# One decoder layer with a routed mixture of experts on one core: the order of small products, of the first output units and of the first and last expert bodies

## What is computed

```python
xn = rms_norm(x, norm1_w)
qa, ka, va, qg, kg, vg, rg, gdown, gate_a, gate_g = split(xn @ w_in)
y_attn = swa_with_sinks(rope(rms_norm(qa)), rope(rms_norm(ka)), va) @ w_attn_branch
gk = log_sigmoid(gdown @ gla_gate_up + gla_gate_bias) / 16
og = rms_norm(gla_chunked(qg, kg, vg, gk)) * silu(rg)
y_gla = og @ w_gla_branch
merged = sigmoid(gate_a) * y_attn + sigmoid(gate_g) * y_gla
h = x + merged @ w_out
xn2 = rms_norm(h, norm2_w)
# one group of 4, then the best two of its 8 experts for each token
y = sum over the chosen experts of weight * ((silu(xn2 @ w_gate) * (xn2 @ w_up)) @ w_down)
out = h + y
```

## Time and profile before

| | us |
|---|---|
| median of 3 runs | 716.54 |
| lowest and highest | 716.33 and 716.84 |
| the profiled execution | 722.02 |
| its span, first to last instruction | 719.8 |
| PE busy within the span | 689.4 |
| DVE, ACT, POOL busy | 378.4, 207.4, 99.6 |

### The profile page before, as it was taken

The page is one execution under the profiler, slowest core; times in us unless marked ns, Lnnn a source line. Parts: engine busy times, 40 slices in busy tenths (PEclk is TensorE's granted clock), DMA queues, the critical chain, the costliest instruction groups (busy, mean ns, idle before and its releaser), DMA issues.

```text
span 719.8 us, 11191 instructions
## 1 busy us (share of the span) xinstructions
PE 689.4 (96%) x4523; PEld 533.1 (74%) x4523; DVE 378.4 (53%) x673; ACT 207.4 (29%) x443; POOL 99.6 (14%) x131
## 2 busy tenths in 40 slices
PE   3999999999999999999989987999999999999997
PEld 1579999878788888888779987665657575756655
DVE  3647224648987777785683454251525344241514
ACT  4355123214443434342433342112020202110111
POOL 1400006857700000000000011110101001010000
PEclk9999999999999999999999995999999999999998
DMA  7413112301111111113345028799999999999922
GB/s 225 136 58 118 60 59 67 110 1 59 59 60 60 59 58 60 59 60 117 117 155 226 30 101 339 294 411 387 412 382 384 404 373 407 392 416 381 416 113 117
DMA packets 49221, 139.32 MB, mean 194 GB/s; under 512 B 6002, under 2 KB 28035, under 8 KB 40980
## 3 DMA queue, kind: packets, MB, share of 16 engines
q1 hardware_dynamic: 46722, 134.36, 49.3%
q0 software_dynamic: 2304, 4.20, 1.7%
q10 hardware_dynamic: 146, 0.07, 0.1%
HBM read 138.61 MB, written 4.19 MB: 198 GB/s over the span
## 4 chain that ended last, share of the span: by engine, by line
PE 88%; DVE 5%; ACT 3%; DMA 2%; issue 2%; POOL 0%; ACTq 0%; DVEq 0%; POOLq 0%
PE bank L861 16%; PE bank L570 13%; PE bank L571 12%; PE bank L572 12%; PE bank L944 9%; PE bank L874 8%; PE bank L771 2%; DVE y_lo L1632 1%; PE bank L833 1%; PE bank L826 1%; PE bank L744 1%; PE bank L770 1%; PE bank L704 1%; PE bank L769 1%; PE bank L708 1%
## 5 line engine op out<-in xcount | busy, mean ns | idle before, releaser
L1327 DVE TENSOR_TENSOR wlo<-wraw,whi 128x2048 fp32r<-128x2048 f32 (+1 forms) x26 | 58.7, 2259 | 31.4 <-ACT whi L1053 31.4
L570 PE MATMUL bank<-whi,xhi 128*128 128x256 f32 (+1 forms) x256 | 73.8, 288 | 0.0
L572 PE MATMUL bank<-whi,xlo 128*128 128x256 f32 (+1 forms) x256 | 72.2, 282 | 0.0
L571 PE MATMUL bank<-wlo,xhi 128*128 128x256 f32 (+1 forms) x256 | 72.1, 282 | 0.0
L570 PE MATMUL bank<-xhi,whi 128*128 128x512 f32 (+2 forms) x176 | 69.3, 398 | 1.6 <-DVE wlo L1327 1.6
L571 PE MATMUL bank<-xlo,whi 128*128 128x512 f32 (+2 forms) x176 | 68.2, 391 | 0.0
L572 PE MATMUL bank<-xhi,wlo 128*128 128x512 f32 (+2 forms) x176 | 67.9, 390 | 0.0
L861 PE MATMUL bank<-wgate,xgT 128*64 128x256 f32 x512 | 59.0, 383 | 0.0
L861 PE MATMUL bank<-wup,xgT 128*64 128x256 f32 x512 | 58.4, 381 | 0.0
L874 PE MATMUL bank<-wdown,hT 128*64 128x512 f32 x256 | 58.1, 595 | 0.0
L1622 DVE SCALAR_TENSOR_TENSOR hg<-bank,pair_w,hs 128x256 f32<-128x256 f32 x16 | 7.7, 484 | 94.2 <-ACT hs L1257 94.2
(11 more groups left out here) (283 smaller groups left out, 1328.6 us busy)
## 6 DMA issues: line engine op xcount, KB each, us to landing
wgate<-in_expert_w_gate SPq DMA_DIRECT2D x32, 1024.0 KB, 8.0
wup<-in_expert_w_up SPq DMA_DIRECT2D x32, 1024.0 KB, 10.2
wdown<-in_expert_w_down SPq DMA_DIRECT2D x32, 1024.0 KB, 16.5
wraw<-in_w_in SPq DMA_DIRECT2D x17, 1024.0 KB, 5.5
wraw<-in_w_out SPq DMA_DIRECT2D x4, 1024.0 KB, 5.2
h<-in_x SPq DMA_DIRECT2D x4, 512.0 KB, 6.3
wraw<-in_w_gla_branch SPq DMA_DIRECT2D x2, 1024.0 KB, 5.0
wraw<-in_w_attn_branch SPq DMA_DIRECT2D x2, 1024.0 KB, 5.1
```

What stands on the lines that cost most here:

```text
L570: nc.tensor.matmul(ps, lhi(k), rhi(k), start=(k == 0), stop=False)
L571: nc.tensor.matmul(ps, lhi(k), rlo(k), start=False, stop=False)
L572: last = nc.tensor.matmul(ps, llo(k), rhi(k), start=False, stop=(k == kt - 1))
L1327: nc.vector.tensor_tensor(w_view(wlo[split_buffer(c)], c), w_view(wraw[c % 2], c), w_view(whi[split_buffer(c)], c).bitcast(F32), ALU.subtr ...
```

## The change

In `schedule()`:

- `("z",)` is split for PE: `("gates", 0)` after `("unit", 1, 1)`, `("gates", 1)` with the meta part after `("unit", 2, 0)`. ACT and DVE do their part of `z` after that, behind `("prep", 3)` instead of ahead of it.
- the units of chunks 8 and 9 are mixed, so that `attT` and `glao` stand behind different full units. The order in which ACT's results for `rg` are counted follows (`RG_ORDER`).

In the programs:

- the means of x for the next block are computed ahead of the scaling of a block;
- the output units (22, 0) and (23, 0) are computed together in `first_outputs`: slices 0 to 6 for both, then slice 7 for both;
- in the first body the transposes for s = 1, `slot_values(1)` and `onehot_transposes` come after the gate and up products of s = 0; DVE and ACT do their parts of it accordingly, and ACT takes the row numbers ahead of the one-hots. DVE builds both one-hots before it counts the rounds;
- in the last body `last_scatter` takes eight banks: the products of s = 0 for six units before the wait for `y_lo` of s = 1;
- `out` is stored in eight halves of blocks instead of four blocks.

```diff
+LAST_BANKS = (0, 1, 2, 3, 4, 5, 6, 7)
...
-    s += [("unit", 0, 0), ("xm", 1), ("unit", 1, 0), ("unit", 0, "m"), ("prep", 2), ("unit", 1, 1), ("z",)]
-    s += [("prep", 3), ("unit", 2, 0), ("unit", 2, 1), ("unit", 2, "m")]
+    s += [("unit", 0, 0), ("xm", 1), ("unit", 1, 0), ("unit", 0, "m"), ("prep", 2), ("unit", 1, 1), ("gates", 0)]
+    s += [("prep", 3), ("unit", 2, 0), ("gates", 1), ("z",), ("unit", 2, 1), ("unit", 2, "m")]
...
-    s += [("prep", 9)]
-    for b in range(NB):
-        s += [("unit", 8, b), ("attT", b)] + ([("kT",)] if b == 0 else [])
-        if b == 1:
-            s += [("qrope", 2)]
-        if b >= 1:
-            s += [("glao", b - 1)]
-    s += [("qrope", 3)]
-    s += [("prep", 10)]
-    for b in range(NB):
-        s += [("unit", 9, b)] + ([("glao", NB - 1)] if b == 0 else []) + [("qT", b), ("ognorm", b)]
+    s += [("prep", 9), ("unit", 8, 0), ("attT", 0), ("kT",), ("unit", 8, 1), ("attT", 1), ("qrope", 2)]
+    s += [("unit", 9, 0), ("glao", 0), ("qT", 0), ("qrope", 3), ("unit", 8, 2), ("attT", 2)]
+    s += [("unit", 9, 1), ("glao", 1), ("qT", 1), ("ognorm", 0), ("unit", 8, 3), ("attT", 3), ("prep", 10)]
+    s += [("unit", 9, 2), ("glao", 2), ("ognorm", 1), ("unit", 9, 3), ("qT", 2), ("glao", 3), ("ognorm", 2), ("qT", 3), ("ognorm", 3)]
...
+            def first_outputs():
+
+                pair = []
+                for c in (WO, WO + 1):
+                    pe.wait_ge(s_lo, c + 1)
+                    ps = banks.take(pe, "unit", ("unit", c, 0))
+                    pair.append((ps, w_view(whi[split_buffer(c)], c), w_view(wlo[split_buffer(c)], c)))
+                for ks in (range(KT - 1), (KT - 1,)):
+                    for ps, wh, wl in pair:
+                        for k in ks:
+                            pe.wait_ge(s_mhi, k + 1)
+                            nc.tensor.matmul(ps[:, 0:CW], mhi[:, k, 0:P], wh[:, k, :], start=(k == 0), stop=False)
+                            nc.tensor.matmul(ps[:, 0:CW], mhi[:, k, 0:P], wl[:, k, :], start=False, stop=False)
+                    for i, (ps, wh, wl) in enumerate(pair):
+                        for k in ks:
+                            pe.wait_ge(s_mlo, k + 1)
+                            last = nc.tensor.matmul(ps[:, 0:CW], mlo[:, k, 0:P], wh[:, k, :], start=False, stop=(k == KT - 1))
+                        if ks[-1] == KT - 1:
+                            last.then_inc(banks.done(("unit", WO + i, 0)), 1)
...
+                def last_scatter(i, n):
+
+                    def add_rows(u, s):
+                        b, half = u // 2, u % 2
+                        for part in (y_hi, y_lo):
+                            last = nc.tensor.matmul(tiles[LAST_BANKS[u]][:, :], onehotT[i % 3][s][:, b, :],
+                                                    part[s][:, half * 512:(half + 1) * 512], start=(s == 0 and part is y_hi),
+                                                    stop=(s == 1 and part is y_lo))
+                        if s == 1:
+                            last.then_inc(s_sc[u % 4], 1)
+
+                    pe.wait_ge(s_ylo[0], n + 1)
+                    for u in range(6):
+                        add_rows(u, 0)
+                    pe.wait_ge(s_ylo[1], n + 1)
+                    for u in range(6):
+                        add_rows(u, 1)
+                    for u in (6, 7):
+                        for s in range(2):
+                            add_rows(u, s)
...
-                row_transposes(0)
-                pe.wait_ge(s_pw, r * BODIES + 1)
-                slot_values(1)
-                for s in range(2):
-                    pe.wait_ge(s_ohT[s], r * BODIES + 1)
-                onehot_transposes()
+                row_transposes(0, (0,))
...
+                    if i == 0:
+                        row_transposes(0, (1,))
+                        pe.wait_ge(s_pw, n + 1)
+                        slot_values(1)
+                        for s in range(2):
+                            pe.wait_ge(s_ohT[s], n + 1)
+                        onehot_transposes()
...
-                        dve.wait_ge(s_sumsq, b + 1)
-                        nc.vector.tensor_scalar(stat[:, b:b + 1], stat[:, b:b + 1], 1.0 / D, EPS,
-                                                ALU.mult, ALU.add).then_inc(s_mean, 1)
+                        for ahead in (0, 1) if b == 0 else (b + 1,):
+                            if ahead < NB:
+                                dve.wait_ge(s_sumsq, ahead + 1)
+                                nc.vector.tensor_scalar(stat[:, ahead:ahead + 1], stat[:, ahead:ahead + 1], 1.0 / D, EPS,
+                                                        ALU.mult, ALU.add).then_inc(s_mean, 1)
```

More of the change, by code:

```diff
@@ L246 @@
 SCHEDULE = schedule()
+RG_ORDER = [step[1:] for step in SCHEDULE if step[0] == "unit" and CHUNKS[step[1]][0] == "rg"]
 def layer_kernel(nc, x, meta_tokens, norm1_w, w_in, q_norm_w, k_norm_w, attn_sinks, gla_gate_up, gla_gate_bias,
@@ L557, in _, with mm3 @@
         def _(pe):
-            def mm3(ps, lhi, llo, rhi, rlo, kt, merged=False):
-                if merged:
-                    for k in range(kt):
-                        pe.wait_ge(s_mhi, k + 1)
-                        nc.tensor.matmul(ps, lhi(k), rhi(k), start=(k == 0), stop=False)
-                        nc.tensor.matmul(ps, lhi(k), rlo(k), start=False, stop=False)
-                    for k in range(kt):
-                        pe.wait_ge(s_mlo, k + 1)
-                        last = nc.tensor.matmul(ps, llo(k), rhi(k), start=False, stop=(k == kt - 1))
-                    return last
+            def mm3(ps, lhi, llo, rhi, rlo, kt):
                 for k in range(kt):
@@ L606, in _ @@
                     name, c0, n, kt = CHUNKS[c]
+                    if c in (WO, WO + 1) and u == 0:
+                        if c == WO:
+                            first_outputs()
+                        continue
                     if u == 0:
@@ L636, in _ @@
                         last = mm3(ps[:, 0:n], cols(mhi, u * P, (u + 1) * P), cols(mlo, u * P, (u + 1) * P),
-                                   cols(wh, 0, n), cols(wl, 0, n), KT, merged=(c0 == 0 and u == 0))
+                                   cols(wh, 0, n), cols(wl, 0, n), KT)
                     last.then_inc(banks.done(step), 1)
-                elif kind == "z":
+                elif kind == "gates":
+                    j = step[1]
                     pe.wait_ge(s_const, (CONST_DMAS - EARLY_DMAS) * 16)
                     pe.wait_ge(*banks.emptied(("unit", 0, 0)))
+                    ps = banks.take(pe, "unit", ("z", j))
+                    nc.tensor.matmul(ps[:, :], gate_up[:, j * P:(j + 1) * P], gdT[:, NM:XC],
+                                     start=True, stop=True).then_inc(banks.done(("z", j)), 1)
+                    if j == 0:
+                        continue
                     pe.wait_ge(*banks.emptied(("unit", 0, "m")))
-                    for j in range(2):
-                        ps = banks.take(pe, "unit", ("z", j))
-                        nc.tensor.matmul(ps[:, :], gate_up[:, j * P:(j + 1) * P], gdT[:, NM:XC],
-                                         start=True, stop=True).then_inc(banks.done(("z", j)), 1)
                     ps = banks.take(pe, "T", "zm")
@@ L1013, in _ @@
                         reload(i, r * BODIES + i)
-            for b in range(NB):
-                for k in (2 * b % 4, 2 * b % 4 + 1):
-                    sp.wait_ge(s_add[k], rounds * (2 * BODIES) + b // 2)
-                sp.dma_start(out[0, b * P:(b + 1) * P, :], h[:, b, :]).then_inc(s_out, 16)
-            sp.wait_ge(s_out, 16 * NB)
+            for u in range(2 * NB):
+                b, cols_ = u // 2, slice(u % 2 * 512, (u % 2 + 1) * 512)
+                sp.wait_ge(s_add[u % 4], rounds * (2 * BODIES) + u // 4)
+                sp.dma_start(out[0, b * P:(b + 1) * P, cols_], h[:, b, cols_]).then_inc(s_out, 16)
+            sp.wait_ge(s_out, 16 * 2 * NB)
         @block.scalar
```

27 lines of the change are left out of this document (16 added, 11 removed).

## The result

| | before | after |
|---|---|---|
| first comparison, median (executions) | 716.69 (4) | 711.06 (4) |
| lowest and highest | 716.33 and 721.97 | 708.66 and 712.88 |
| beside the experiments, median | 720.92 (31), 721.87 (11), 720.78 (17) | 710.7 (6) |
| the profiled execution, its span | 722.02, 719.8 | 712.88, 711.0 |

A forecast was written before the change was run, and what follows sets the result against it. PE, busy 689.4 of 719.8 us, was taken as the bound, so only its waits and clock could change; 0.3 + 1.7 + 1.4 + 2.3 + 0.4 + 3.5 = 9.6 us off 716.54 gave 706.9, range 704.0 to 711.0.

The forecast's parts named there:

- The base: Whole kernel: the saving of 9.6 us is taken off the median 716.54, which lies 5.5 us under the profiled execution.
- Start: 0.3: Scalings of x: the mean computed ahead saves 0.3 us, as GpSimd's power stands still beside DVE's scaling; range to 1.6.
- more than the sum: Rival: GpSimd runs beside the scaling (1.3 more) and the clock rises early in the first body (0.7 more): 704.9; chance 0.13.
- Gate 1.7: Gate's wide products moved apart: the clock's fall from 47.5 to 50.9 goes, saving 1.7 us; range 0 to 1.7.
- gated attention 1.4: Chunks 8 and 9, units mixed: the clock's fall at 153.3 goes, saving 1.4 us; 0 with a new fall elsewhere.
- Output units 2.3: Units (22, 0) and (23, 0) together: unit (24, 0) starts 2.3 us earlier despite a new 1.7 us wait before hT; range 0.6 to 2.3.
- First body 0.4 saved: First expert body: gate and up of s = 0 ahead of the s = 1 transposes saves 0.4 us; 1.1 saved to 1.0 lost.
- L: First expert body: low-clock time in gate and up of s = 0, taken as 2.5 us; alternatives 1.15 and 5.5.
- Last body 3.5: Last expert body: the 2.1 us wait for y_lo and the 1.7 fall go; DVE's last sum starts 3.5 us earlier.
- The prediction's own sign of being wrong: Wrong if the clock falls where it was 1.00, PE waits for weights in the expert loop, or last eight sums exceed 5 us.
- Slower: Rival: attention from 180 to 330 us, shifted about 3.4 us earlier, gets new falls at 1.7 us each; chance 0.03.
- chance is in it: Rival, falls stay or move: each worth 1.4 to 1.7 us; two left 710.3, chance 0.25; all four 713.4, chance 0.05.

The follow-up runs named there:

- before_look: The kernel before, unchanged, profiled a second time; 720.96 us in a single execution.
- after_again: The changed kernel once more, unchanged; median 710.7 us beside 721.87 for the kernel before.
- fill_start: The changed kernel with idle PE products at the start, 6 ahead of a bank wait and 5 ahead of the first unit; 709.16 us.
- fill_gather: The changed kernel with idle PE products where PE waits for the choice of experts and the gather; 710.04 us.
- the medians of the four: Four kernels, each the kernel before with one part alone: last body, output units, gated attention, gate; medians 716.4, 717.86, 715.67, 715.36 us.
- outputs_only: The kernel before with only output units (22, 0) and (23, 0) computed together; median 717.86 us, ratio to before 0.998.
- gla_only: The kernel before with only the units of chunks 8 and 9 mixed; median 715.67 us, ratio to before 0.994.
- gate_only: The kernel before with only the gate's two wide products moved apart; median 715.36 us, ratio to before 0.995.
- before_late: The kernel before with seven idle PE products ahead of chunk 5's first unit; 719.7 us beside 720.78, ratio 1.000.

## Why the prediction was right or wrong

- **The base.** "The median lies 5.5 us under that execution, and I take the same saving off it." This step failed. Falls were treated as fixed parts of the kernel, so a trace with all five of them can't belong to a median of 716.5; that the two differed by 5.5 us, three falls' worth, was the sign. From the usual 721.2 the sum gives 711.6, and 711.0 was measured (median of the ten executions of after). That the saving of the profiled pair, 9.1, lies so near 9.6 is partly luck: the first body missed by 1.1 and the gate by 0.5, and 0.7 that the forecast had not counted came behind the last sums.
- **Start: 0.3, measured 1.3.** The mechanism was right, GpSimd stands still beside the scaling. Mis-sized was the chain behind it: each block was given its own power after its own scaling, while the second power runs right behind the held-up one and is ready before the next scaling ends. So 1.0 us more than forecast came here, though not by the way of "more than the sum", a power running beside the whole scaling. In the profiled execution the kernel gave 0.8 of the 1.3 back, since its first unit ran at half clock to 28.3: the earlier trace rows has 24.29 for the start of that unit, after has 22.32, but ACT's copy `whi` of chunk 2, behind it, starts only 0.5 us earlier than before.
- **Gate 1.7, gated attention 1.4.** Right in kind, and near in size, in the profiled pair: between the copies `whi` of chunks 2 and 4 the start moved from 0.5 to 1.66 us ahead of before, and between those of chunks 9 and 11 from 1.66 to 3.25. That makes 1.2 and 1.6. No fall came in eight profiles each. Over many executions such a term is worth its price times the chance that the fall comes, 5 of 6 and 3 of 6 here; and before can have more than one in the attention, as `before_look` shows.
- **Output units 2.3, measured 2.0.** The new wait in front of `hT` was there as described, 1.2 us and not 1.7, since PE was done with both units 0.9 us later than worked out (371.83 - 1.18 = 370.65, against 373.0 less the 3.25 by which all came earlier) and DVE's sum came 0.4 later (371.36 against 374.24 - 3.25). No fall followed in eight profiles.
- **First body 0.4 saved, measured 0.7 lost.** The step that failed is "I take 2.5" for L. The clock rose at 444.8, 4.9 us after the gate products began, and 454.9 + 4.9 / 2 = 457.4 against 456.69 is that loss. The formula held. The value was taken from the first unit of before; the other profiles with this order have 3.0 (`after_again`) and 4.1 (`fill_start`). At 3.6 us it neither saves nor loses, by the same formula.
- **Last body 3.5, measured 3.5.** Down ended 4.6 us earlier than before, the last sum 8.1. The eight sums took 4.87 us. The fall that was counted in it came in 2 of 6 unchanged profiles. Where it doesn't come, the part is worth 1.8 us in the forecast's own working. What follows the sums took 4.35 instead of 5.04 us, since it lay at full clock and not at 0.68, by luck: in `after_again` the clock falls 3.5 us behind the last sum.
- **The rivals.** At the four places no fall stayed. A low stretch of 10.2 us lay at the start in two profiles with the changed start (after and `fill_gather`), where the first unit paid for it. The prediction's own sign of being wrong, a fall where the clock was at 1.00, is met by after at 18.1 us as far as the view of before goes. "Slower" is out: the attention from 180 to 330 us kept a clock of 1.00 in after. The reading that "chance is in it" stood only in a rival and should have stood in every term.
- **Open.** What decides whether a gap brings a fall, and what each part is worth by itself: the medians of the four add up to 18.4 us, their ratios to about 12, with the whole at 10.4 to 11.2. A part can gain at a place that it doesn't touch: from the choice of experts on, the clock is low for 13.7 us in the profiles of `outputs_only`, `gla_only` and `gate_only`, for 17.1 or 20.5 in those of before, and for 17.1 in after. Each part moves all that follows in time, and `before_late` hints that this changes the falls, but no run shows it.

## What to carry over

Compare the mean granted clock of a profiled execution with that of the timed ones before a saving is taken off a median: here a short fall of the clock in one trace was a chance, not a fixed cost, and its term is price times frequency. Measure the kernel before beside the changed one, in the same series. Gaps and groups of small products are still worth spreading out: with that done, no fall came at these four places in eight profiles each. Where PE must wait ahead of dense work, idle products in the wait, fewer than fill it even at half clock, are worth trying: together with the old order of the first body they brought 1.8 to 3.4 us on top of this change, depending on how one counts, and which of the two parts brought how much is not shown.

## What the runs showed of the hardware

- The same kernel, with the same waits to a tenth of a microsecond, has the clock fall at different places in different executions (before and `before_look`). Its times lie up to 10.5 us apart (715.03 to 725.56), and go with the mean clock (0.983 to 0.969). The Trainium skill (TensorE: Matmul & The Clock Gate, Part 1) says that the monitor behind the clock looks at PE in a window that runs freely; the traces agree in so far as the falls don't keep to the program.
- A fall can follow a stretch in which PE is busy nearly all the time: in `before_look` the clock falls at 151.6 and rises at 158.4, and PE was busy for 4.47 of the 4.60 us from 147.0 to 151.6, with full products to 147.7 and small ones (`attT`, `glao`) after that.
- GpSimd's power of one column takes 0.55 us alone and 1.52 when it starts behind a scaling by DVE of two SBUF tiles that is still running. One that started 0.06 us ahead of such a scaling took 0.54, and the scaling its usual 1.28.
